# One block of attention on VectorE: the older head's output moved into the middle of a vector-matrix chunk

## The chip, the cores and the metric

The kernel runs on one core of one Trainium2 chip. The metric is the device time of one execution in microseconds, taken as the median over runs. The engines are TensorE (PE in the profile), VectorE (DVE), ScalarE (ACT), GpSimd (POOL) and the queue engine SyncE (SP); each follows its own list of instructions and waits for the others on semaphores.

## The reference, cut to what matters

Two transformer-like blocks are computed on a sequence of 512 tokens of width 1024. The change touches the attention of the first block: 16 heads of 64, causal, with a forgetting gate, and beside it a modulation vector that is a product of one vector with a large weight matrix.

```python
def forgetting_attention(q, k, v, log_f):
    ...
        logits = jnp.einsum('bqhd,bkhd->bhqk', q[:, q0:q1], k[:, :q1],
                            preferred_element_type=jnp.float32) * scale
        logits = logits + (cum[:, :, q0:q1, None] - cum[:, :, None, :q1])
        mask = jnp.arange(q0, q1)[:, None] >= jnp.arange(q1)[None, :]
        logits = jnp.where(mask, logits, -jnp.inf)
        probs = jax.nn.softmax(logits, axis=-1)
        outs.append(jnp.einsum('bhqk,bkhd->bqhd', probs.astype(v.dtype), v[:, :q1]))
    return jnp.concatenate(outs, axis=1)
...
        mod = jnp.einsum('bd,de->be', c_act, w_ada[l]) + b_ada[l]
        sh1, sc1, g1, sh2, sc2, g2 = [m[:, None, :] for m in jnp.split(mod, 6, axis=-1)]
```

## The kernel before, in words

Everything is written out by hand: each engine has its own list, and the order on it is the order of the Python code. The projections of the first block are computed with each matrix split into a high and a low part; ACT makes the high part of a weight tile (`hi`, line 745), POOL subtracts it from the raw tile to get the low part (`lo`, line 551). One weight tile is four POOL instructions of 128x512 in a row, called a burst here. TensorE then does three products per tile (lines 1705 to 1707).

The first attention is a pipeline of 18 steps, `for s in range(18)`, on every engine. In step s the heads are at different stages:

- PE first transposes the probabilities of head s-2 (`probs_t`, line 1844, ten small matmuls; before the last two it waits until the output of head s-3 has been read out of the shared bank). Then it computes a projection tile for a later pair of heads (24 matmuls, lines 1705 to 1707), then the product of probabilities and values of head s-2 (`values`, lines 1854 to 1861), then waits for the four exponentials of head s-1, sums the columns of the finished modulation chunk (`late_columns`, line 1819, in steps that follow a chunk) and computes the scores of head s (lines 2037 and 2038). Steps 14 to 17 have a part of the output projection in place of a projection tile, and it waits for the last query and key splits.
- ACT copies the transposed probabilities (line 830), computes the four exponentials of head s-1 (line 792), which need the negated row maxima from DVE, and in even steps below 14 makes the high part of the next weight tile; the POOL burst follows that. In odd steps POOL has no burst. ACT also sends the reciprocals through memory to spread them over partitions (`send_inverse`, `fetch_inverse`).
- DVE begins with the mask and the row maxima of head s-1 (lines 1460, 1177 and 1181), then the low part of a query or key tile (lines 1446 and 1449). In the steps of `LATE_STEP` it then sums a chunk of the modulation product (`weigh`, one multiply on line 1264 and seven multiply-adds on line 1270, each of 128x256 and reading two tiles of the on-chip memory, `arena` and `tmp`). In the middle of the chunk, ahead of the fourth multiply-add from the end, it takes the reciprocal of the row sums of head s-1 (`inverse`, line 1188). The last work of a step is the output of head s-2 (`output`, line 1195): two multiplies of 64x256, each reading the product from a bank and the spread reciprocals from the arena. It waits for `values` of the same step and for the reciprocals.

The steps with a chunk are 1, 2, 3, 5 to 11 and 13; steps 4, 12 and 14 on have none. Below, the middle of a chunk is the point right behind line 1188, and its second half the four multiply-adds after it.

Of the kernel before, what the change touches and what calls it, by code (L numbers as in the profile page):

```python
# [115 lines left out]
LATE_STEP = (1, 2, 3, 5, 6, 7, 8, 9, 10, 11, 13)  # L116
# [22 lines left out]
def build(nc, x, c, w_ada, b_ada, w_in, conv_w, conv_b, dt_bias, a_log, d_skip, ssm_norm_w, f_bias,  # L139
# [3 lines left out]
    with ExitStack() as ctx:  # L143
# [204 lines left out]
        def own(half):  # L348

            return slice(HD * half, HD * half + HD)  # L350
# [5 lines left out]
        def by_query(features, side):  # L356

            return features.rearrange("p (q n) -> p q n", q=TB)[:, (slice(0, 4, 3), slice(1, 3))[side]]

        def inverse_rows(h, side):  # L360

            rows_ = (inv_row if h < 16 else inv_row2)[own(h % 2)]
            return rows_.rearrange("p (n q) -> p q n", q=TB)[:, (slice(0, 4, 3), slice(1, 3))[side]]

        def value_out(side):

            return bank[3][own(side), 256:512].rearrange("p (q n) -> p q n", q=2)

        def att_pair(h):

            return att[:, h // 2] if h < 16 else att2[:, h // 2 % 2]
# [773 lines left out]
        def _(dve):  # L1145
# [37 lines left out]
            def inverse(h):  # L1183

                dve.wait_ge(p_made, 4 * h + 4)
                if h:
                    dve.wait_ge(inv_out, 16 * h)
                dve.reciprocal(rinv[:, 1], rsum[:, h % 2]).then_inc(inv_made, 1)

            def output(h):  # L1190

                dve.wait_ge(o_mm, h + 1)
                dve.wait_ge(inv_in, 16 * (h + 1))
                for side in range(2):
                    last = dve.tensor_tensor(by_query(att_pair(h)[own(h % 2)], side), value_out(side), inverse_rows(h, side), ALU.mult)
                last.then_inc(o_made, 1)

            def att_low(pair):

                dve.wait_ge(a_hi_made, T_ATT + pair + 1)  # L1200
                dve.scalar_tensor_tensor(a_lo[0][:, pair], att[:, pair], v1[:, V_ATT + pair:V_ATT + pair + 1],
                                         a_hi[0][:, pair].bitcast(F32), ALU.mult, ALU.subtract).then_inc(a_lo_made, 1)
# [57 lines left out]
            def weigh(acc, src, before, signal, middle=None, between=None):  # L1260

                for wait in before:
                    dve.wait_ge(*wait)
                link(dve.tensor_scalar(acc, src(0), cact[:, 0:1], None, ALU.mult))
                for k in range(1, KT):
                    if k == KT // 2 and middle:
                        dve.wait_ge(*middle)
                    if k == KT // 2 and between is not None:
                        inverse(between)
                    ins = dve.scalar_tensor_tensor(acc, src(k), cact[:, k:k + 1], acc, ALU.mult, ALU.add)  # L1270
                    if k < KT - 1:
                        link(ins)
                    else:
                        ins.then_inc(signal, 1)

            def late_ada(n, between=None):

                before = [(late_in[n % 2], 16 * (n // 2 + 1))] + ([(col_mm, 4 + n - 3)] if n >= 4 else [])
                weigh(late_place(n), lambda k: late_slot(n)[:, 256 * k:256 * k + 256], before, late_sum, between=between)

            def start():
                dve.wait_ge(c_made, 1)
                weigh(tmp[:, 0], lambda k: ada[:, 0, k], [(ada_half[0], 16)], ada_sum, (ada_half[1], 16))
                dve.wait_ge(vecs_t, 1)
                dve.tensor_copy(vec[:].rearrange("p a b -> p (a b)"), bank[7][:, 0:256]).then_inc(vecs_made, 1)
                dve.wait_ge(vecs_made, 1)
                for n in range(1, 4):
                    before = [(ada_in[n], 16)] + ([(col_mm, n - 1)] if n >= 2 else [])
                    weigh(tmp[:, n % 2], lambda k: ada[:, n, k], before, ada_sum)
                dve.wait_ge(col_mm, 4)  # L1290
                dve.tensor_tensor(mod[:, 0:8], bank[7][:, 256:264], v0[:, V_BADA:V_BADA + 8], ALU.add)
                dve.scalar_tensor_tensor(mod[:, 8:16], bank[7][:, 264:272], 1.0, v0[:, V_BADA + 8:V_BADA + 16], ALU.add, ALU.add).then_inc(mod_made, 1)
                dve.wait_ge(landed[U_XBC % 2], 16)
                for half in range(2):
                    cols = slice(1024 * half, 1024 * half + 1024)
                    dve.tensor_copy(w_hi[:, U_XBC % 2, cols], raw[:, U_XBC % 2, cols]).then_inc(w_hi_made, 1)
                split_affine(M_H, 0, lambda k: mod[:, 8 + k:9 + k])

            def late_mod():
                link(dve.tensor_scalar(mod[:, 16:24], mod[:, 16:24], 1.0, None, ALU.add))  # L1300
                link(dve.tensor_scalar(mod[:, 32:48], mod[:, 32:48], 1.0, None, ALU.add))

                for n, factor in ((48, mod[:, 32:40]), (64, v1[:, V_N1:V_N1 + KT])):
                    for m in range(2):
                        v = V_LN[(n - 48) // 16] + KT * m
                        link(dve.tensor_tensor(mod[:, n + KT * m:n + KT * m + KT], v1[:, v:v + KT], factor, ALU.mult))
                dve.tensor_tensor(mod[:, 56:64], mod[:, 56:64], mod[:, 24:32], ALU.add).then_inc(late_made, 1)
# [131 lines left out]
            def split_lo(n, b):  # L1439

                for half in range(2):
                    rows_ = own(half)
                    dve.wait_ge(qk_hi, 4 * n + 2 * half + 2)
                    if n % 2:
                        hc, lh = k_pair(n // 2, half)
                        dve.tensor_tensor(lh[rows_], bank[b][rows_, :], hc[rows_].bitcast(F32), ALU.subtract).then_inc(qk_lo, 1)
                    else:
                        hh, l1 = q_pair(n // 2, half)
                        dve.scalar_tensor_tensor(l1[rows_], bank[b][rows_, :], HD ** -0.5, hh[rows_].bitcast(F32),
                                                 ALU.mult, ALU.subtract).then_inc(qk_lo, 1)  # L1450

            def fox_maxima(h):

                dve.wait_ge(s_mm, h + 1)
                if h == 14:
                    dve.wait_ge(col_mm, 4 + N_LATE)
                    link(dve.tensor_tensor(mod[:, 16:48], bank[6][:, ADA_COL:ADA_COL + 32], v0[:, V_BADA + 16:V_BADA + 48], ALU.add))
                for b, o, n in ((4, 256, 2), (6, 128, 1), (5, 384, 1)):
                    diagonal = bank[b][:, o:o + n * P].rearrange("p (a k) -> p a k", a=n)
                    last = dve.tensor_tensor(diagonal, diagonal, hide.unsqueeze(1).broadcast_to([P, n, P]), ALU.add)  # L1460
                link(last)
                maxima(h, lambda q: bank[SB[q][0]][:, SB[q][1]:SB[q][1] + (q + 1) * P])
# [76 lines left out]
            for s in range(18):  # L1539
                if 1 <= s < 17:  # L1540
                    fox_maxima(s - 1)
                if 3 <= s < 15:
                    split_lo(s + 1, (s - 1) % 2)
                if s == 15:
                    for pair in range(3):
                        att_low(pair)
                elif s == 16:
                    late_mod()
                if s in LATE_STEP:
                    late_ada(LATE_FIRST + LATE_STEP.index(s), s - 1)  # L1550
                elif 1 <= s < 17:
                    inverse(s - 1)
                if s == 16:
                    att_low(3)
                    att_low(4)
                elif s == 17:
                    att_low(5)
                if s >= 2:
                    output(s - 2)
            att_low(6)  # L1560
            att_low(7)
# [700 lines left out]
```

## Time and profile before

| | |
|---|---|
| median of 3 runs | 1418.73 us (1417.94 to 1420.17) |
| the profiled execution's own time | 1418.4 us |
| its span in the trace | 1416.7 us |
| mean granted TensorE clock | 0.996 of full speed |
| PE busy | 1367.4 us, 97% of the span |
| DVE busy | 695.4 us, 49% |
| ACT busy | 547.0 us, 39% |
| POOL busy | 692.1 us, 49% |

Times are in microseconds from the start of the span. The attention of the first block lies between 257 and 430 us. The time of the execution is 1.7 us more than its span; the median of the runs is 0.3 us more than the profiled execution's time.

### The profile page before, as it was taken

What the parts mean: (1) busy time and instruction counts of PE and PEld (TensorE: products, weight loads), DVE (VectorE), ACT (ScalarE), POOL (GpSimd) and SP (SyncE); (2) the same over time, 40 slices, a digit from 0 to 9 for tenths busy, and PEclk for the clock granted to TensorE, in tenths of its full rate; (3) what the DMA queues carried; (4) which work ended last, traced back from release to release, by engine and by line L of the source; (5) the groups of instructions that cost most, each with busy time, mean ns of one, the idle gap of its engine ahead of it and who ended that gap; (6) DMA issues with size and microseconds to landing.
All of it is one profiled execution on the core that took longest, in us unless ns stands there. A gap on an engine that the chain in (4) does not pass through costs nothing.

```text
span 1416.7 us, 17285 instructions
## 1 busy us (share of the span) xinstructions
PE 1367.4 (97%) x6567; PEld 1122.0 (79%) x6567; DVE 695.4 (49%) x1005; ACT 547.0 (39%) x793; POOL 692.1 (49%) x544
## 2 busy tenths in 40 slices
PE   2999999999999999999999997999999999999999
PEld 2888778878778778888888886887788888888887
DVE  6676978689843672131324447348623213132231
ACT  0635454566663252231332316325525323142230
POOL 0453864332346664455445554753644445445442
PEclk9999999999999999999999999999999999999999
DMA  9353435745323423322232232243132322322231
GB/s 334 118 122 109 100 122 176 216 134 162 105 72 122 148 90 101 107 89 89 90 117 89 89 104 76 97 124 92 45 119 64 115 89 89 112 95 89 89 104 74
DMA packets 132248, 158.58 MB, mean 112 GB/s; under 512 B 9468, under 2 KB 93712, under 8 KB 131936
## 3 DMA queue, kind: packets, MB, share of 16 engines
q1 hardware_dynamic: 123760, 146.95, 32.9%
q10 hardware_dynamic: 6240, 5.40, 1.8%
q0 software_dynamic: 2192, 5.49, 1.2%
q8 instruction: 34, 0.56, 0.2%
q14 instruction: 22, 0.18, 0.0%
HBM read 153.47 MB, written 2.26 MB: 110 GB/s over the span
## 4 chain that ended last, share of the span: by engine, by line
PE 86%; DVE 7%; POOL 3%; issue 2%; ACT 1%; DMA 1%; SPq 0%; DVEq 0%; ACTq 0%; POOLq 0%
PE bank L1705 26%; PE bank L1707 25%; PE bank L1706 25%; POOL w_lo L551 3%; DVE tmp L1270 2%; PE bank L1844 1%; PE bank L2222 1%; DMA arena<-in_w_ada_dram 1%; PE bank L1854 1%; PE bank L1829 1%; PE bank L2037 1%; PE bank L1819 1%; PE bank L1857 1%; PE bank L2038 1%; PE bank L1981 1%
## 5 line engine op out<-in xcount | busy, mean ns | idle before, releaser
L551 POOL TENSOR_TENSOR w_lo<-raw,w_hi 128x512 fp32r<-128x512 f32 x428 | 589.9, 1410 | 593.7 <-ACT w_hi L745 592.5
L1705 PE MATMUL bank<-w_hi,a_hi 128*128 128x512 f32 x928 | 364.6, 393 | 8.5 <-DVE a_lo L1163 6.0
L1707 PE MATMUL bank<-w_hi,a_lo 128*128 128x512 f32 x928 | 361.9, 390 | 0.0
L1706 PE MATMUL bank<-w_lo,a_hi 128*128 128x512 f32 x928 | 361.9, 390 | 0.0
L745 ACT ACTIVATE w_hi<-raw 128x2048 fp32r<-128x2048 f32 x107 | 204.7, 1914 | 360.9 <-PE bank L1707 357.9
L1705 PE MATMUL bank<-a_hi,w_hi 128*128 128x512 f32 x800 | 315.6, 394 | 3.4 <-DVE a_lo L1163 2.5
L1706 PE MATMUL bank<-a_lo,w_hi 128*128 128x512 f32 x800 | 312.1, 390 | 0.0
L1707 PE MATMUL bank<-a_hi,w_lo 128*128 128x512 f32 x800 | 312.0, 390 | 0.0
L1705 PEld LDWEIGHTS bank<-w_hi,a_hi 128*128 128x128 f32 x928 | 174.7, 188 | 46.4 <-DVE a_lo L1163 6.2
L1707 PEld LDWEIGHTS bank<-w_hi,a_lo 128*128 128x128 f32 x928 | 174.6, 188 | 36.8
L1706 PEld LDWEIGHTS bank<-w_lo,a_hi 128*128 128x128 f32 x928 | 174.7, 188 | 35.5
L1705 PEld LDWEIGHTS bank<-a_hi,w_hi 128*128 128x128 f32 x800 | 150.6, 188 | 35.5 <-issue 2.7
L1707 PEld LDWEIGHTS bank<-a_hi,w_lo 128*128 128x128 f32 x800 | 150.6, 188 | 32.0
L1706 PEld LDWEIGHTS bank<-a_lo,w_hi 128*128 128x128 f32 x800 | 150.7, 188 | 30.5 <-issue 0.2
L1251 DVE TENSOR_TENSOR tmp<-arena 128x512 f32<-128x512 f32 x64 | 64.3, 1005 | 190.1 <-ACT arena L843 190.0
L843 ACT ACTIVATE arena<-bank 128x512 f32<-128x512 f32 x64 | 38.4, 599 | 211.1 <-PE bank L1707 204.7
L1694 DVE SCALAR_TENSOR_TENSOR arena<-bank,st,arena 128x512 f32<-128x512 f32 x32 | 24.0, 751 | 144.6 <-PE bank L1707 144.6
L1270 DVE SCALAR_TENSOR_TENSOR tmp<-arena,cact,tmp 128x256 f32<-128x256 f32 (+1 forms) x140 | 88.0, 629 | 4.7
L1151 DVE TENSOR_TENSOR a_lo<-tmp,a_hi 128x512 fp32r<-128x512 f32 x64 | 67.6, 1057 | 7.2
L1593 DVE TENSOR_TENSOR arena<-bank,arena 128x512 f32<-128x512 f32 x24 | 16.6, 692 | 109.6 <-PE bank L1707 109.6
L792 ACT ACTIVATE arena<-bank,mxs 128x128 f32<-128x128 f32 (+1 forms) x96 | 49.5, 534 | 35.0 <-DVE mxs L1181 35.0
L845 ACT ACTIVATE a_hi<-arena 128x512 fp32r<-128x512 f32 x64 | 40.5, 633 | 2.0
(248 smaller groups left out, 1246.7 us busy)
## 6 DMA issues: line engine op xcount, KB each, us to landing
raw<-in_w_mlp_dram SPq DMA_DIRECT2D x32, 1024.0 KB, 5.2
raw<-in_w_in_dram SPq DMA_DIRECT2D x24, 1024.0 KB, 5.2
arena<-in_w_ada_dram SPq DMA_DIRECT2D x18, 1024.0 KB, 6.5
raw<-in_w_ff_in_dram SPq DMA_DIRECT2D x16, 1024.0 KB, 5.4
raw<-in_w_ff_out_dram SPq DMA_DIRECT2D x16, 1024.0 KB, 5.0
raw<-in_w_out_dram SPq DMA_DIRECT2D x12, 1024.0 KB, 5.5
raw<-in_w_in_dram SPq DMA_DIRECT2D x16, 512.0 KB, 6.0
arena<-in_w_ada_dram SPq DMA_DIRECT2D x3, 2048.0 KB, 18.0
```

Of the source, the lines that this page charges most:

```text
L551: last = pool.tensor_tensor(w_lo[:, u0 % 2, cols], raw[:, u0 % 2, cols], w_hi[:, u0 % 2, cols].bitcast(F32), ALU.subtract)
L745: act.activation(w_hi[:, u0 % 2], raw[:, u0 % 2], ACT.Copy).then_inc(w_hi_made, 1)
L792: act.activation(dst[:, QO[q]:QO[q] + n], src(q), ACT.Exp, bias=mxs[:, h % 2, q:q + 1], accum_out=rsum[:, h % 2, q:q + 1]).then_inc(p_made, 1)
L843: act.activation(rl[:, k % 2], bank[4 * b + j][:], ACT.Relu).then_inc(evac[b], 1)
L845: act.activation(a_hi[1][:, k], rl[:, k % 2], ACT.Square).then_inc(a_hi_made, 1)
L1151: dve.tensor_tensor(a_lo[buf][:, k], tmp[:, m0 % 2], a_hi[buf][:, k].bitcast(F32), ALU.subtract)\
L1251: dve.tensor_tensor(tmp[:, k % 2], rl[:, k % 2], rl[:, k % 2], ALU.mult).then_inc(tile_made, 1)
L1270: ins = dve.scalar_tensor_tensor(acc, src(k), cact[:, k:k + 1], acc, ALU.mult, ALU.add)
L1694: dve.scalar_tensor_tensor(x1[:, t, part], bank[4 * b + t][:], st[:, 12 + t:13 + t], x1[:, t, part], ALU.mult, ALU.add).then_inc(evac[b], 1)
L1705: pe.matmul(out_, hi_a, hi_b, start=start, stop=False)
L1706: pe.matmul(out_, hi_a, lo_b, start=False, stop=False)
L1707: return pe.matmul(out_, lo_a, hi_b, start=False, stop=stop)
```

## The change

The output of head s-2 moves within step s on DVE: in a step with a chunk it now stands in the middle of the chunk, behind the reciprocals of head s-1, and no longer behind the chunk. In steps without a chunk it stays where it was. `inverse(between)` is called with `between` = s-1, so `output(between - 1)` is `output(s - 2)`; in step 1 there is nothing to put out. No instruction is added or removed, no other engine's list changes, and no tile changes its place.

```diff
@@ -1267,6 +1267,8 @@
                         dve.wait_ge(*middle)
                     if k == KT // 2 and between is not None:
                         inverse(between)
+                        if between:
+                            output(between - 1)
                     ins = dve.scalar_tensor_tensor(acc, src(k), cact[:, k:k + 1], acc, ALU.mult, ALU.add)
                     if k < KT - 1:
                         link(ins)
@@ -1555,7 +1557,7 @@
                     att_low(4)
                 elif s == 17:
                     att_low(5)
-                if s >= 2:
+                if s >= 2 and s not in LATE_STEP:
                     output(s - 2)
             att_low(6)
             att_low(7)
```

Below is DVE's order from the middle of the chunk in step 2 to the row maxima that open step 3, before the change (line 1270 is the multiply-add, 1195 the output, 1460 the mask of step 3).

```order
L1188 RECIPROCAL rinv<-rsum 128x4
L1270 SCALAR_TENSOR_TENSOR tmp<-arena,cact,tmp 128x256 x4
L1195 TENSOR_TENSOR arena<-bank,arena 64x2x128
L1195 TENSOR_TENSOR arena<-bank,arena 64x256
L1460 TENSOR_TENSOR bank<-bank,masks 128x256
```

The same stretch of DVE after the change, where the lines behind the edit carry numbers that are two higher.

```order
L1188 RECIPROCAL rinv<-rsum 128x4
L1195 TENSOR_TENSOR arena<-bank,arena 64x2x128
L1195 TENSOR_TENSOR arena<-bank,arena 64x256
L1272 SCALAR_TENSOR_TENSOR tmp<-arena,cact,tmp 128x256 x4
L1462 TENSOR_TENSOR bank<-bank,masks 128x256
```

The two output multiplies went ahead of the second half of the chunk; steps 3, 5 to 11 and 13 read the same way.

The second place is DVE after the change from the reciprocal of step 12, which has no chunk, to the maxima that open step 14 (line 1451 and 1448 are the query and key splits).

```order
L1188 RECIPROCAL rinv<-rsum 128x4
L1195 TENSOR_TENSOR arena<-bank,arena 64x2x128
L1195 TENSOR_TENSOR arena<-bank,arena 64x256
L1462 TENSOR_TENSOR bank<-bank,masks 128x256
L1462 TENSOR_TENSOR bank<-bank,masks 128x128 x2
L1177 TENSOR_REDUCE rinv<-bank 128x1 x4
L1181 TENSOR_SCALAR mxs<-rinv 128x4
L1451 SCALAR_TENSOR_TENSOR q_split<-bank,q_split 64x512 x2
L1264 TENSOR_SCALAR tmp<-arena,cact 128x256
L1272 SCALAR_TENSOR_TENSOR tmp<-arena,cact,tmp 128x256 x3
L1188 RECIPROCAL rinv<-rsum 128x4
L1195 TENSOR_TENSOR arena<-bank,arena 64x2x128
```

In step 12 nothing moved; in step 13 the output stands in the chunk again, ahead of the maxima of step 14 and the key split on which PE's step 14 waits.

## Rows read from the trace of the kernel before

**Rows 1.** The first line of the page: busy time of each engine.

```profile
PE 1367.4 (97%) x6567; PEld 1122.0 (79%) x6567; DVE 695.4 (49%) x1005; ACT 547.0 (39%) x793; POOL 692.1 (49%) x544
```

**Rows 2.** By stretch: length, busy PE, PEld, DVE, ACT, POOL, granted clock, DMA share, GB/s.

```profile
257.00:304.00 47.00, 47.00 (x282) 38.93 (x283) 37.35 (x91) 30.01 (x72) 14.91 (x17) 1.00 0.59 159
304.00:365.00 61.00, 58.97 (x363) 48.07 (x362) 58.22 (x128) 40.23 (x94) 18.93 (x19) 1.00 0.56 169
```

**Rows 3.** Waits of PE between 257 and 430 us: total, times, longest.

```profile
PE bank L1844 <- DVE arena L1195: 1.9, 2, 1.5
PE bank L1705 <- DVE k_split L1446: 0.8, 1, 0.8
PE bank L1844 <- ACT arena L830: 0.5, 2, 0.3
```

**Rows 4.** DVE's timeline, steps 6 to 10: start, duration, instruction.

```profile
310.52 3.99 DVE L1270 SCALAR_TENSOR_TENSOR tmp<-arena,cact,tmp 128x256 f32<-128x256 f32 x4
...
315.80 0.83 DVE L1460 TENSOR_TENSOR bank<-bank,masks 128x256 f32<-128x256 f32 x3
...
321.93 2.02 DVE L1270 SCALAR_TENSOR_TENSOR tmp<-arena,cact,tmp 128x256 f32<-128x256 f32 x4
...
325.25 0.83 DVE L1460 TENSOR_TENSOR bank<-bank,masks 128x256 f32<-128x256 f32 x3
...
331.29 0.18 DVE L1188 RECIPROCAL rinv<-rsum 128x4 f32<-128x4 f32 x1
331.38 2.96 DVE L1270 SCALAR_TENSOR_TENSOR tmp<-arena,cact,tmp 128x256 f32<-128x256 f32 x4
...
345.13 0.83 DVE L1460 TENSOR_TENSOR bank<-bank,masks 128x256 f32<-128x256 f32 x3
```

**Rows 5.** POOL's timeline: bursts of steps 2 and 8.

```profile
272.41 5.19 POOL L551 TENSOR_TENSOR w_lo<-raw,w_hi 128x512 fp32r<-128x512 f32 x4 [14.18 <-ACT w_hi L745]
...
332.79 5.20 POOL L551 TENSOR_TENSOR w_lo<-raw,w_hi 128x512 fp32r<-128x512 f32 x4 [6.50 <-ACT w_hi L745]
```

**Rows 6.** DVE's timeline ahead of the attention: whole chunks of seven.

```profile
219.89 7.28 DVE L1270 SCALAR_TENSOR_TENSOR tmp<-arena,cact,tmp 128x256 f32<-128x256 f32 x7
...
235.89 3.61 DVE L1270 SCALAR_TENSOR_TENSOR tmp<-arena,cact,tmp 128x256 f32<-128x256 f32 x7
```

**Rows 7.** POOL's timeline in the same stretch.

```profile
220.63 5.74 POOL L551 TENSOR_TENSOR w_lo<-raw,w_hi 128x512 fp32r<-128x512 f32 x4 [7.91 <-ACT w_hi L745]
```

**Rows 8.** DVE's timeline, step 2 and the opening of step 3.

```profile
270.62 0.18 DVE L1188 RECIPROCAL rinv<-rsum 128x4 f32<-128x4 f32 x1 [0.45 <-ACT arena L792]
...
273.20 1.22 DVE L1195 TENSOR_TENSOR arena<-bank,arena 64x256 f32<-64x256 f32 x2 [0.47 <-PE bank L1857]
275.10 0.83 DVE L1460 TENSOR_TENSOR bank<-bank,masks 128x256 f32<-128x256 f32 x3 [0.68 <-PE bank L2038]
```

**Rows 9.** PE's timeline, steps 2, 3, 7 and 13, single instructions.

```profile
271.85 0.43 PE L1854 MATMUL bank<-arena 128*64 128x256 f32 x1
...
281.54 0.43 PE L1854 MATMUL bank<-arena 128*64 128x256 f32 x1
...
282.77 0.27 PE L1819 MATMUL bank<-ones,tmp 128*128 128x1 f32 x1
...
322.96 0.38 PE L1819 MATMUL bank<-ones,tmp 128*128 128x1 f32 x2
...
380.86 0.43 PE L1854 MATMUL bank<-arena 128*64 128x256 f32 x1
```

**Rows 10.** ACT's timeline: exponentials of step 7, weight tile of step 8.

```profile
318.58 0.37 ACT L792 ACTIVATE arena<-bank,mxs 128x128 f32<-128x128 f32 x1 [1.84 <-DVE mxs L1181]
...
320.51 0.21 ACT L792 ACTIVATION_READ_ACCUMULATOR arena<-bank,mxs 128x1 f32 x1
...
330.76 1.95 ACT L745 ACTIVATE w_hi<-raw 128x2048 fp32r<-128x2048 f32 x1
```

**Rows 11.** DVE's timeline, step 13.

```profile
380.90 0.18 DVE L1188 RECIPROCAL rinv<-rsum 128x4 f32<-128x4 f32 x1
```

## The prediction

> **What bounds the kernel now.** I read the page first, for the balance of the engines: PE is busy for 97% of the span [rows 1], so a change matters by what it adds to or takes from PE's waits. The change stands in the first attention alone, so next came the busy time by stretch. From 304 to 365 us, the steps 6 to 11, PE is busy 58.97 of 61 us and DVE 58.22 [rows 2]. The reader is to see that DVE is as full there as PE: the two bound this stretch together. From 257 to 304 us PE has no gap at all. Then came PE's waits from 257 to 430 us [rows 3]. They are 3.2 us in all: 1.9 for an output of DVE (line 1195), 0.8 for a key split of DVE, 0.5 for a copy by ACT. That is the most that any better order on DVE can give back here.
>
> Then I read DVE's timeline. A step begins with the row maxima: at 315.80 in step 7, 325.25 in step 8 and 345.13 us in step 10 [rows 4]. So the odd step 7 takes 9.45 us, and the two steps 8 and 9 take 19.88, the even one of them 10.43 if step 9 is like step 7. PE's own step is 9.69 us (values of step 2 at 271.85, of step 3 at 281.54) [rows 9]. Two steps of DVE, 19.88 us, are longer than two of PE, 19.38. The even steps are longer because their second half of a chunk takes 2.96 us (step 8) or 3.99 (step 6) where the odd step 7 needs 2.02 [rows 4]. What stands beside it is POOL: in step 8 its burst starts at 332.79 [rows 5], inside the second half that runs from 331.38 to 334.34.
>
> **The price of a burst to a chunk.** Ahead of the attention there are whole chunks with and without a burst. Seven multiply-adds take 3.61 us alone and 7.28 with a burst of four across them [rows 6, 7]. So a held multiply-add costs (7.28 - 3.61) / 4 = 0.92 more, 1.44 in place of 0.52. The output is not held: it took 1.22 us at 273.20, in the midst of the burst of 272.41 to 277.60 [rows 5, 8].
>
> The Trainium skill has a rule that speaks against this change ("SBUF — State Buffer", section on the two separate sides): DVE and GpSimd share a pair of ports as a lock and not as bandwidth, and a DVE instruction with two inputs in that memory waits out a running GpSimd instruction. The trace agrees, 1.44 us in place of 0.52, also in that the output, with one input in a bank, is free. By the rule alone each held multiply-add would wait for what is left of one POOL instruction, about the same sum.
>
> **The change part by part.** It adds and removes nothing. It moves ten outputs of 1.22 us (1.26 with the gap) ahead of four multiply-adds. That does two things: the output now waits in the chunk where PE's product isn't there yet, and the second half starts 1.26 us later or more, which in the even steps is into POOL's burst.
>
> Where the burst lies, relative to the maxima of an even step: the exponentials start 2.78 behind the maxima (315.80 to 318.58), the weight tile on ACT 2.0 behind that, the burst 2.03 after it (330.76 to 332.79) [rows 4, 5, 10], so 6.8 us in all when ACT waits for nothing else. The middle of the chunk is 6.22 behind the maxima (331.29 + 0.18 - 325.25) [rows 4], the second half now 7.5. So the burst starts 0.7 us ahead of the second half, and all four multiply-adds are held: the first for the rest of a quarter of a burst, about 0.9, three at 1.44, in all 5.2 us.
>
> Step 2. The middle is reached at 270.80, but PE only begins the values at 271.85 and the output can start 1.35 later, at 273.20, as now [rows 8, 9]. It ends at 274.42, and the second half starts in a burst that ends near 277.9: one at 0.9, two at 1.44, one free, 4.3 us. The maxima of step 3 start at 278.8 and not at 275.10 [rows 8]. The exponentials end 4.9 behind the maxima (315.80 to 320.72) [rows 4, 10], at 283.7. PE wants them at 282.77 [rows 9]: a new wait, **+0.9 us**. Queued behind it are the scores of head 3, and DVE's next maxima wait for these. Step 4 has no chunk, so DVE catches up, but PE's 0.9 stays.
>
> Step 5, like step 13: in step 13 the middle is reached at 381.08, PE begins the values at 380.86 and the output can start at 382.2 [rows 9, 11]. DVE stands for 1.1 us. It enters step 6 later by 0.9 + 1.1 = 2.0.
>
> Step 6: the second half takes 5.2 in place of 3.99, so the maxima of step 7 come 3.2 to 3.3 later, at 319.1, and the exponentials end at 324.0. PE would be there at 322.96, less the 1.5 us that it now waits for the output in this step [rows 3], which is gone since the output comes early, plus 0.9: at 322.4. It waits until 324.0, so it stands **+1.1 us** behind today. The gain that the move can have is in this term, and the maxima eat it.
>
> Steps 8 and 10: from here PE follows DVE, since scores need exponentials and these the maxima. Two steps of DVE take 19.88 - 2.96 + 5.2 = 22.1 us. That is 2.2 more than now, twice: **+4.4 us**. In both, PE's wait moves from the output (even steps) to the exponentials (line 792, odd steps).
>
> Steps 12 to 14: step 12 has no chunk and DVE catches up with PE again. In step 13 it stands 1.1 us for the values, so the key split in step 14 comes 1.1 later, and PE waits for that split already (0.8 us, [rows 3]). **+1.0 us**, a tenth less for a short wait at the opening of step 14 that this covers.
>
> Sum: 1.1 (which holds the 0.9 of step 3) + 4.4 + 1.0 = 6.5 us. Behind step 14 PE is the bound again and waits for little, so nothing gives the loss back. Against the profiled execution's 1418.4 us this is 1424.9; the median of the runs shown is 0.3 above that execution, so I say **1425.2 us**.
>
> Bounds of the one unknown, the second half under a burst (the trace has none of four held in an even step). From below: no more than it costs now, 3.99 and 2.96. Then DVE's two steps stay at 19.88 and only the 1.1 waits count: PE is about 1.0 ahead at step 7 (1.5 gained, 0.5 waited) and loses 1.0 in step 14, so 0.0 to +0.5. From above: four whole quarters, 4 x 1.44 = 5.8. Then each even step has 0.6 more, step 2 too, some 2 us in all: +8.5. I take 5.2, as the chunk of [rows 6] is the same instruction under the same burst.
>
> **The rivals.**
> - *No difference.* The second half in a burst costs no more than now, since POOL starts later or in other gaps. Against it: all four fall behind the start of the burst by rows. Time 1418.7 to 1419.2. Chance 0.10.
> - *Faster.* PE's waits for the output (1.9), the split (0.8) and ACT's copy (0.5) all vanish: 1415.5 us. It is one mechanism: the early output frees the shared bank before PE wants it, while DVE's later maxima stay within the slack of the exponentials. That slack is 322.96 - 320.72 = 2.2 us in step 7, less the 1.5 that PE gains [rows 9, 10]; so the maxima may be 0.7 late at most, and that is where it decides. By my sum they are 3.3 late. Chance 0.03.
> - *Slower, but half.* Only two of four are held in steps 6 to 10 (3.9 us): two steps of DVE take 20.8, PE loses 0.9 twice, and little in step 7, so some +2.5, 1421.2. What would speak for it is that POOL starts later than by rows. Chance 0.12.
> - *Slower, all four at full price*, 1427.2 us. Chance 0.10.
> - *The forecast*, 1423 to 1426.5 by itself. Chance 0.65.
>
> **How the numbers follow.** The predicted time is the forecast's. The range takes in the half case's upper side and the full price, 1421.3 to 1427.5, and leaves out some 0.18. About 0.2% (2.8 us) is what a measurement of this kernel can tell from no change: so slower by more than that holds the forecast, the full price and half of the half case, 0.82; within it 0.15; faster 0.03.
>
> **What the changed profile would show.** From 304 us on, DVE's second halves in steps 6, 8 and 10 at 5.2 us or near it, and in step 2 at 4.3 (now 2.02). Maxima of odd steps 3 us and more behind today's, with 22 us from step 7 to step 9. PE's waits for line 1195 gone, and in their place waits of 1.5 to 3 us ahead of lines 1819 and 2037 for ACT's line 792 in steps 7, 9 and 11, 0.9 in step 3. A wait of near 2 us for the key split in step 14. DVE idle for 1.1 us ahead of line 1195 in steps 5 and 13 and 2.4 in step 2. Behind 400 us, all shifted by one amount. The prediction is wrong if the second halves stay under 4 us, or if PE's waits for the exponentials stay under 1 us.

## The result and the profile after

The change makes the kernel slower by 0.8%: 1430.01 us (1428.53 to 1431.11, 4 runs) against 1418.40 us (1417.94 to 1420.17), ratio 1.0079 [1.0068, 1.0091]. The profiled execution took 1428.53 us. The same kernel timed again beside the one before gave 1428.24 us against 1418.47, ratio 1.0067 [1.0053, 1.0081] (e12_after_again below). So the loss is 9.8 to 11.6 us where 6.8 was forecast, and both medians lie above the range.

The first lines of the page, for [rows 1]:

```profile
span 1426.8 us, 17285 instructions
PE 1370.0 (96%) x6567; PEld 1125.4 (79%) x6567; DVE 706.5 (50%) x1005; ACT 547.9 (38%) x793; POOL 694.5 (49%) x544
```

The same instructions on every engine, 10.1 us more span, and 11.1 us more busy time on DVE though no work was added to it. Grouped by line, DVE's instructions between 257 and 440 us, first before and then after the change (line, engine, operation, shapes, count | busy us, mean ns | idle before):

```profile
L1270 DVE SCALAR_TENSOR_TENSOR tmp<-arena,cact,tmp 128x256 f32<-128x256 f32 x77 | 40.9, 531 | 2.4
L1195 DVE TENSOR_TENSOR arena<-bank,arena 64x256 f32<-64x256 f32 x32 | 19.6, 611 | 15.4 <-PE bank L1857 14.9
```

```profile
L1272 DVE SCALAR_TENSOR_TENSOR tmp<-arena,cact,tmp 128x256 f32<-128x256 f32 x77 | 48.6, 632 | 2.5
L1195 DVE TENSOR_TENSOR arena<-bank,arena 64x256 f32<-64x256 f32 x32 | 19.5, 610 | 21.8 <-PE bank L1859 21.4
```

The multiply-adds of the chunks alone cost 7.7 us more; DVE stands 21.8 us ahead of the output, where it stood 15.4. PE's waits in the same stretch, for [rows 3]:

```profile
PE bank L1821 <- ACT arena L792: 7.0, 4, 2.8
PE bank L1707 <- DVE k_split L1448: 3.3, 1, 3.3
PE bank L1846 <- DVE arena L1195: 0.4, 1, 0.4
```

The wait for the output has gone from 1.9 to 0.4 us, and 7.0 us of waits for the exponentials have come. DVE's timeline of steps 2 and 6 to 10 after the change, for [rows 4, 8]:

```profile
273.18 1.22 DVE L1195 TENSOR_TENSOR arena<-bank,arena 64x256 f32<-64x256 f32 x2 [2.40 <-PE bank L1859]
274.33 4.25 DVE L1272 SCALAR_TENSOR_TENSOR tmp<-arena,cact,tmp 128x256 f32<-128x256 f32 x4
...
313.84 5.27 DVE L1272 SCALAR_TENSOR_TENSOR tmp<-arena,cact,tmp 128x256 f32<-128x256 f32 x4
319.14 0.83 DVE L1462 TENSOR_TENSOR bank<-bank,masks 128x256 f32<-128x256 f32 x3
...
326.66 2.05 DVE L1272 SCALAR_TENSOR_TENSOR tmp<-arena,cact,tmp 128x256 f32<-128x256 f32 x4
328.74 0.83 DVE L1462 TENSOR_TENSOR bank<-bank,masks 128x256 f32<-128x256 f32 x3
...
336.18 5.22 DVE L1272 SCALAR_TENSOR_TENSOR tmp<-arena,cact,tmp 128x256 f32<-128x256 f32 x4
341.44 0.83 DVE L1462 TENSOR_TENSOR bank<-bank,masks 128x256 f32<-128x256 f32 x3
```

POOL's bursts beside the two held halves, for [rows 5]:

```profile
313.25 5.58 POOL L551 TENSOR_TENSOR w_lo<-raw,w_hi 128x512 fp32r<-128x512 f32 x4 [7.38 <-ACT w_hi L745]
...
335.56 5.57 POOL L551 TENSOR_TENSOR w_lo<-raw,w_hi 128x512 fp32r<-128x512 f32 x4 [8.08 <-ACT w_hi L745]
```

The burst starts 0.6 us ahead of the second half in steps 6 and 8, and all four multiply-adds of it are held: 5.27 and 5.22 us. The odd step 7 has none beside it, 2.05. The maxima of step 7 start at 319.14, 3.34 us behind [rows 4], and those of step 9 come 22.30 us after them. PE's row at the end of step 7's wait, for [rows 9]:

```profile
324.13 0.61 PE L1821 MATMUL bank<-ones,tmp 128*128 128x1 f32 x4 [2.14 <-ACT arena L792]
```

That is 1.17 us behind the 322.96 of before. Up to here the prediction holds to 0.2 us. What it didn't have begins with the granted clock. By stretch, for [rows 2] (us, busy PE, PEld, DVE, ACT, POOL, granted clock, DMA share, GB/s), first before and then after:

```profile
343.00:352.00 9.00, 9.00 (x53) 7.49 (x55) 8.58 (x21) 6.98 (x16) 1.06 (x2) 1.00 0.43 133
367.00:376.00 9.00, 9.00 (x58) 7.46 (x57) 4.92 (x13) 8.75 (x20) 3.47 (x3) 1.00 0.09 19
394.00:402.00 8.00, 8.00 (x48) 6.50 (x47) 5.03 (x13) 5.11 (x15) 0.00 (x0) 1.00 0.53 151
```

```profile
343.00:352.00 9.00, 6.19 (x37) 5.48 (x34) 8.51 (x20) 4.25 (x12) 1.06 (x2) 0.81 0.69 237
367.00:376.00 9.00, 7.70 (x43) 6.72 (x40) 8.51 (x21) 5.45 (x14) 1.05 (x2) 0.81 0.50 178
394.00:402.00 8.00, 4.75 (x16) 3.49 (x15) 4.44 (x9) 7.13 (x15) 4.96 (x4) 0.79 0.05 5
```

0.81 over 9 us, and 0.79 over 8, are 3.4 us at TensorE's lower level, 1.2 GHz, and the rest at 2.4. They begin at 346.8, 370.6 and 398.0 us: the first two 0.3 and 1.9 us behind the end of PE's waits in steps 9 and 11, the third 0.5 us ahead of the end of its wait in step 14. Before the change there is none in the attention. The second thing stands at the opening of step 14, on DVE and on POOL:

```profile
393.25 0.83 DVE L1462 TENSOR_TENSOR bank<-bank,masks 128x256 f32<-128x256 f32 x3
...
395.84 1.21 DVE L1181 TENSOR_SCALAR mxs<-rinv 128x4 f32<-128x4 f32 x1
396.96 1.40 DVE L1448 TENSOR_TENSOR k_split<-bank,k_split 64x512 fp32r<-64x512 f32 x2
```

```profile
395.76 4.96 POOL L551 TENSOR_TENSOR w_lo<-raw,w_hi 128x512 fp32r<-128x512 f32 x4 [3.07 <-ACT w_hi L745]
```

```profile
398.41 0.79 PE L1707 MATMUL bank<-w_hi,a_hi 128*128 128x512 f32 x1 [3.25 <-DVE k_split L1448]
```

The negation of the maxima, four elements a row, takes 1.21 us. The burst began 0.08 us ahead of it and holds it, and the key split, for which PE waits, is queued behind. Before the change the negation was over before the burst came:

```profile
386.90 0.17 DVE L1181 TENSOR_SCALAR mxs<-rinv 128x4 f32<-128x4 f32 x1
```

```profile
388.06 5.01 POOL L551 TENSOR_TENSOR w_lo<-raw,w_hi 128x512 fp32r<-128x512 f32 x4 [3.08 <-ACT w_hi L745]
```

But the trace of before has the same hold at another place, where it could have been read ahead of the change. Step 4 has no chunk, and the negation that opens step 5 comes so early that it runs into the last quarter of step 4's burst: it takes 0.60 us and ends with that quarter, near 297.65. The one that opens step 13, behind step 12 without a chunk, takes 0.60 us too.

```profile
297.07 0.60 DVE L1181 TENSOR_SCALAR mxs<-rinv 128x4 f32<-128x4 f32 x1
```

```profile
292.61 5.04 POOL L551 TENSOR_TENSOR w_lo<-raw,w_hi 128x512 fp32r<-128x512 f32 x4 [6.52 <-ACT w_hi L745]
```

The table is PE's lateness against the kernel before, in us, and the experiments are read by it. It is the start of PE's first score matmul of steps 7, 11 and 13 (line 2039 after the change), and of its first value matmul of step 14, less the same start in the trace of before; each trace is shifted so that the values of step 2 fall together. The stretches at 1.2 GHz are those in the attention, each 3.4 us long. In e4_clean_after the value matmul of step 14 falls into the stretch; once that is over, PE is 2.5 us late.

| kernel | step 7 | 11 | 13 | 14 | at 1.2 GHz, near | median less its before |
|---|---|---|---|---|---|---|
| after | 1.19 | 6.09 | 7.73 | 11.37 | 347, 371, 398 | +11.6 |
| after, again (e12) | 1.14 | 6.01 | 7.65 | 11.27 | 346, 370, 398 | +9.8 |
| e3_fill | 1.17 | 6.02 | 6.02 | 9.88 | 397 | +9.0 |
| e8_fill_all | 1.15 | 5.99 | 5.99 | 8.29 | none | +9.0 |
| e6_s14 | 1.20 | 6.16 | 7.81 | 10.62 | 326, 370, 397 | +9.7 |
| e13_fill_s14 | 1.13 | 5.97 | 5.97 | 7.23 | none | +8.1 |
| e10_only13 | 0 | 0 | 0 | 3.60 | 389 | +2.9 |
| e1_even | 2.24 | 7.91 | 9.84 | 9.37 | 329 | +9.6 |
| e2_odd | 2.43 | 9.53 | 9.53 | 11.80 | 317, 341, 365 | +12.2 |
| e4_clean_after | -1.88 | -1.90 | -1.36 | 2.15 | 390 | +1.9 |
| e5_clean_before | -1.88 | -2.85 | -2.85 | -3.31 | none | -3.0 |
| e9_clean_after_s14 | -1.35 | -0.99 | -0.35 | 0.89 | none | +0.6 |
| e11_wait | 2.30 | 8.19 | 8.19 | 8.21 | 326, 350 | +8.3 |

### The profile page after: what moved, and what is told of

It reads as the page before. It is cut to its first block, busy times and chain, and to the rows that moved or that the text cites. A ratio compares the mean times of both kernels' runs of the same rounds, so it can differ in the third digit from the quotient of the medians.

```text
span 1426.8 us, 17285 instructions
## 1 busy us (share of the span) xinstructions
PE 1370.0 (96%) x6567; PEld 1125.4 (79%) x6567; DVE 706.5 (50%) x1005; ACT 547.9 (38%) x793; POOL 694.5 (49%) x544
## 4 chain that ended last, share of the span: by engine, by line
PE 84%; DVE 9%; POOL 3%; issue 2%; ACT 2%; DMA 1%; SPq 0%; DVEq 0%; POOLq 0%; ACTq 0%
PE bank L1707 25%; PE bank L1709 25%; PE bank L1708 25%; DVE tmp L1272 3%; POOL w_lo L551 3%; PE bank L1846 1%; DMA arena<-in_w_ada_dram 1%; PE bank L2224 1%; PE bank L1831 1%; DVE rinv L1177 1%; PE bank L1856 1%; DVE arena L1195 1%; PE bank L1859 1%; PE bank L1821 1%; PE bank L1983 1%
## 5 line engine op out<-in xcount | busy, mean ns | idle before, releaser
L1272 DVE SCALAR_TENSOR_TENSOR tmp<-arena,cact,tmp 128x256 f32<-128x256 f32 (+1 forms) x140 | 95.8, 684 | 4.8
L1195 DVE TENSOR_TENSOR arena<-bank,arena 64x256 f32<-64x256 f32 x48 | 29.3, 610 | 28.1 <-PE bank L1859 27.5
```

## The experiments

Line numbers shift by up to twelve with the edits; the words of a row tell the instruction.

**e1_even and e2_odd: half of the change each.** One table picks the steps in which the output stands in the chunk; e1_even has the steps 2, 6, 8 and 10, e2_odd has 3, 5, 7, 9, 11 and 13.

```diff
+MOVED = (2, 6, 8, 10)
...
-                        if between:
+                        if between and between + 1 in MOVED:
                             output(between - 1)
...
-                if s >= 2 and s not in LATE_STEP:
+                if s >= 2 and s not in MOVED:
                     output(s - 2)
```

> The output stands in the middle of the chunk in the even steps 2, 6, 8 and 10 alone; in the odd ones it stays behind the chunk. Burst theory (multiply-adds held by POOL's bursts are the cost, and bursts come in even steps alone): the second halves of steps 6, 8 and 10 take 5.2 us as in the changed kernel, and an odd step is no shorter than now, so the loss is all there: 1427 to 1431 us. Rival (the cost is DVE standing in the chunk for PE's product, in steps 3, 5 and 13 as much as in step 2): only step 2 still waits, so most of the loss goes, 1420 to 1422 us.

Measured: 1428.14 us (1427.78 to 1430.01), ratio 1.0068 [1.0054, 1.0082]. PE's waits between 257 and 440 us:

```profile
PE bank L1847 <- DVE arena L1196: 5.9, 5, 1.7
PE bank L1822 <- ACT arena L793: 4.6, 4, 1.3
```

The even half has the held second halves (4.76 us in steps 6 and 8), and in odd steps the output stays last and is now late by them, so PE waits for it, 5.9 us. Both kinds of wait stand side by side, and it loses 1.8 us more up to step 11 than the whole change.

> The output stands in the middle of the chunk in the odd steps 3, 5, 7, 9, 11 and 13 alone, where POOL has no burst. Burst theory in its plain form: no multiply-add is newly held, so only the 1.1 us waits of steps 5 and 13 count: 1419 to 1421 us. A less plain form: DVE comes later into each even step by that wait, its second half meets more of the burst (3 held in place of 1 or 2) and PE waits both for the output in even steps and for the exponentials in odd ones: up to 1425 us. Rival (standing for PE's product is the cost): six of the ten moves are here, so more than half of the 11 us stays.

Measured: 1430.81 us (1429.27 to 1431.88), ratio 1.0087 [1.0073, 1.0101]. PE's waits, and then rows of DVE's timeline:

```profile
PE bank L1847 <- DVE arena L1196: 7.6, 4, 2.7
PE bank L1708 <- DVE k_split L1449: 3.3, 1, 3.3
```

```profile
312.02 3.81 DVE L1273 SCALAR_TENSOR_TENSOR tmp<-arena,cact,tmp 128x256 f32<-128x256 f32 x4
315.85 1.21 DVE L1196 TENSOR_TENSOR arena<-bank,arena 64x256 f32<-64x256 f32 x2
...
325.78 1.23 DVE L1196 TENSOR_TENSOR arena<-bank,arena 64x256 f32<-64x256 f32 x2 [2.47 <-PE bank L1860]
```

I had thought this half nearly free, as no burst lies in odd steps, and had allowed 1425 us at most. It is as slow as the whole change, and that theory falls; what holds for this half is the rival, that DVE stands for PE's product. PE opens the odd step with a wait for the output that DVE still puts last in the even step; its values are late by it; DVE, which now wants these values in the middle of the odd chunk, stands 2.47 us, the rest of its chunk and the next even step come later by it, and so does the output for which PE waits next. The two engines wait for each other in turn. And the burst still reaches two multiply-adds of the even chunk, 3.81 us in steps 6, 8 and 10 (3.99, 2.96 and 2.96 before). All multiply-adds together take only 1.7 us more than before, so in this half it is the stands, with the stretches at 1.2 GHz beside them, and not the held instructions that make PE 9.5 us late at step 11:

```profile
L1273 DVE SCALAR_TENSOR_TENSOR tmp<-arena,cact,tmp 128x256 f32<-128x256 f32 x77 | 42.6, 553 | 2.6
```

So the odd and the even half of the move aren't two parts of a sum: each is dearer alone, and the whole change is cheaper than either up to step 11.

> The output in the middle in odd steps once more, one look for the place of its half-clock stretches: as in its first run if the stretches are tied to PE's waits.

The kernel that ran under this label is that of e2_odd, line for line, so it is a second execution of it, 1433.62 us: 9.47 us late at step 11, 13.00 at step 14, with a fourth stretch at 1.2 GHz near 403 us. It tells nothing else.

**e3_fill and e8_fill_all: the clock apart from the waits.** PE gets matmuls that nobody reads, into a bank that is free, just ahead of its waits, so that it is busy there and still can't go on earlier. e3_fill has them in steps 3, 7, 9 and 11, e8_fill_all also at the opening of step 14 (the loop over 11, which e3_fill hasn't). They add work that the reference doesn't have.

```diff
+FILL = {3: 3, 7: 8, 9: 11, 11: 11}
...
+                for m in range(11 if s == 14 else 0):
+                    pe.matmul(bank[7][:], w_hi[:, 1, 0:P], a_hi[0][:, m % KT], start=True, stop=True)
                 if s >= 2:
                     probs_t(s - 2, prob)
...
+                for m in range(FILL.get(s, 0)):
+                    pe.matmul(bank[7][:], w_hi[:, 0, 0:P], a_hi[0][:, m % KT], start=True, stop=True)
                 if 1 <= s < 16:
                     pe.wait_ge(p_made, 4 * s)
```

> The changed kernel, with 3, 8, 11 and 11 extra matmuls of 128x512 (0.23 us each, into a bank that is free there) on PE ahead of its wait for the exponentials in steps 3, 7, 9 and 11, where PE stands for 0.8 to 2.8 us; what they compute is overwritten. Clock theory (the half-clock stretches at 347, 371 and 398 us follow PE's idle time and carry some 4 us of the loss): with PE kept busy the first two go away and the time falls by 2.5 to 3 us, to about 1427, although PE does more. Rival (the clock is no part of it, the waits alone are the loss): no gain, 1430 or up to 1 us more where a filler outlasts a wait.

> The changed kernel with extra matmuls ahead of PE's waits in steps 3, 7, 9 and 11 as before, and 11 more at the opening of step 14, where PE later stands 3.3 us for the key split; what they compute is overwritten. Clock theory: no half-clock stretch is left in the attention, and the time is that of the waits alone: the 6.5 us of the forecast plus 1.0 for the held negation in step 14, 1425 to 1426.5. Rival (filling one place only moves the stretch elsewhere, or PE is late by the fillers): 1427.5 as with four places, or above.

Measured: e3_fill 1427.51 us (1425.52 to 1430.00), ratio 1.0065 [1.0052, 1.0079]; e8_fill_all 1427.87 us (1426.10 to 1430.21), 1.0064 [1.0050, 1.0078]. By stretch, e3_fill:

```profile
367.00:376.00 9.00, 8.89 (x49) 7.38 (x48) 8.54 (x21) 5.29 (x14) 1.05 (x2) 1.00 0.46 153
394.00:402.00 8.00, 5.78 (x27) 4.24 (x27) 2.31 (x4) 4.96 (x14) 4.53 (x4) 0.79 0.27 56
```

and e8_fill_all:

```profile
394.00:402.00 8.00, 7.26 (x44) 5.56 (x44) 3.39 (x6) 4.80 (x13) 4.43 (x4) 1.00 0.28 58
```

With the filler the clock stays at 1.00 behind the waits, and PE's lateness at step 11 is what it was (6.02 and 5.99, 6.09 without). But from step 11 to 13 nothing is lost any more, where the change lost 1.64 us, and step 14 loses 2.30 us in e8_fill_all where e3_fill loses 3.86. So the stretch near 371 us costs 1.6 us and the one near 398 costs 1.6; the one near 347 costs 0.1 at most, because DVE is the bound there and PE would have waited anyway. The medians don't show all of it: e8_fill_all's whole kernel is no faster than e3_fill's, and slower than the 1425 to 1426.5 us expected. In its profiled execution the 1.2 GHz stretch behind the next layer norm, near 506 us, is 6.8 us long and not 3.4, and the end is 0.9 us later than the lateness at step 14 and the earlier start of its trace (0.65 us) account for.

**e6_s14 and e13_fill_s14: the held negation.** POOL's burst at the opening of step 14 waits until DVE has the negation of that step; e13_fill_s14 has this and all the filler.

```diff
+                if u == U_WO1 + 1:
+                    pool.wait_ge(mx_made, 14)
                 lo(u)
```

> The changed kernel, with POOL's burst of step 14 alone held back until the maxima of head 13 are negated. In the changed kernel that burst starts 0.08 us ahead of the negation (line 1181), which then takes 1.21 us and not 0.17, and PE waits for the key split behind it. If that hold is a term of the loss, the time falls by 1.0 us, or by 2 to 2.5 if the shorter wait of PE also saves the half-clock stretch at 398 us. If the key split is late for DVE's chunk alone: no change beyond 0.3 us.

> The changed kernel with all extra matmuls (steps 3, 7, 9, 11 and 14) and POOL's burst of step 14 behind the negation. If the loss in the attention is the sum of held multiply-adds and DVE's wait in step 13 (8.3 us by the version with fillers alone, less 1.0 for the held negation) and the rest is clock, PE is 7.2 to 7.5 us behind the kernel before at the end of the attention, with no half-clock stretch between 260 and 430 us; 1425 to 1427 us, the later stretches as they fall. If the two terms aren't apart (the negation's hold hides under something else), 8.3 us.

Measured: e6_s14 1427.74 us (1426.01 to 1428.26), ratio 1.0064 [1.0050, 1.0078]; e13_fill_s14 1426.53 us (1424.02 to 1427.05), 1.0051 [1.0037, 1.0065], beside 1428.24 for the change. DVE and POOL in e6_s14:

```profile
395.50 0.17 DVE L1183 TENSOR_SCALAR mxs<-rinv 128x4 f32<-128x4 f32 x1
```

```profile
395.75 4.98 POOL L551 TENSOR_TENSOR w_lo<-raw,w_hi 128x512 fp32r<-128x512 f32 x4 [3.40 <-DVE mxs L1183]
```

The negation is back at 0.17 us, the wait for the key split goes from 3.3 to 2.2 us, and between e8_fill_all and e13_fill_s14, which differ in this alone, PE's lateness falls by 1.06 us. What is left, 7.23, is 5.97 up to step 11 and 1.26 in step 14. DVE's stand in step 13 is 0.80 us of these 1.26; most of the rest is the negation that opens step 13, 0.94 us under the end of a burst where it took 0.60 before.

**e10_only13: the move in one step.** `MOVED = (13,)`.

> The output in the middle of the chunk in step 13 alone. The forecast's term for it: DVE stands 1.1 us for PE's product and the key split of step 14 comes that much later, +1.0 us. With the held negation of step 14, as in the changed kernel, +2.0, and with a half-clock stretch behind PE's longer wait up to +3.5: 1420.5 to 1422. Without either: 1419.5.

Measured: 1421.74 us (1419.89 to 1422.91), ratio 1.0021 [1.0012, 1.0030]. PE's wait and the clock, 384 to 393 us:

```profile
PE bank L1708 <- DVE k_split L1449: 3.3, 1, 3.3
```

```profile
384.00:393.00 9.00, 5.75 (x20) 4.34 (x19) 5.74 (x13) 8.25 (x18) 5.01 (x5) 0.81 0.06 16
```

Ten outputs moved cost 11.4 us by the end of the attention, and one of them alone costs 3.6: the same wait of 3.3 us, the negation again at 1.21 us, the same stretch at 1.2 GHz, which begins 0.5 us ahead of the wait's end. No second half is held longer here. It is the term of step 13 with both of its unforeseen followers, in a kernel that is otherwise on time.

**e4_clean_after, e5_clean_before and e9_clean_after_s14: bursts out of DVE's way.** POOL's bursts of steps 2 to 12 wait for the end of DVE's chunk where the step has one, and the last quarter of each for the negated maxima; e4_clean_after is the changed kernel with this, e5_clean_before the kernel before with it, e9_clean_after_s14 adds the condition of e6_s14.

```diff
...
+                if chunk is not None:
+                    pool.wait_ge(late_sum, chunk + 1)
                 for part in range(4):
+                    if part == 3 and head is not None:
+                        pool.wait_ge(mx_made, head + 1)
...
+                s = 2 * (u - U_QK1)
+                if 2 <= s < 14:
+                    lo(u, chunk=LATE_FIRST + LATE_STEP.index(s) if s in LATE_STEP else None, head=s)
```

> The changed kernel, with POOL's bursts of the attention moved in time: in an even step with a chunk the burst waits until the chunk is summed, and its last quarter until the next maxima are negated, so that it lies beside DVE's bank-reading work. Burst theory: the second halves go back to 2.05 us, DVE's two steps to 19 us, the new waits for the exponentials and with them the half-clock stretches go, and what is left is the 1.1 us wait of step 13: 1417.5 to 1420 us. Rival (early output and DVE's wait for PE are the cost by themselves): the loss stays over 5 us, above 1424.

> The kernel before (output behind the chunk in every step), with POOL's bursts moved in time as in the clean version of the changed kernel. Burst theory: no multiply-add is held, DVE's two steps (19 us) are shorter than PE's (19.4), PE's waits for the output in the opening of steps 7, 9 and 11 go: 1415 to 1417 us, and it is faster than its counterpart with the moved output by the 1 us that DVE stands for PE's product in step 13. Rival (PE's waits in the kernel before come from elsewhere): 1418 to 1419.

> The changed kernel with POOL's bursts moved in time and the burst of step 14 held back behind the negation as well. Burst theory: what was left of the loss with clean bursts (2 us) was this hold and the half-clock stretch at 390 us that followed the 3.2 us wait for the key split: 1417.3 to 1418.8. Rival (that rest is DVE standing for PE's product in step 13): no gain over 1420.5.

Measured: e4_clean_after 1420.46 us (1418.88 to 1423.65), ratio 1.0020 [1.0009, 1.0030]; e5_clean_before 1415.09 us (1413.77 to 1416.78), 0.9978 [0.9969, 0.9988]; e9_clean_after_s14 1419.46 us (1417.97 to 1423.27), 1.0008 [0.9999, 1.0017]. The two changed kernels are slower than expected by 0.5 and 0.7 us, and the executions of e4_clean_after fall into two groups (1418.9 to 1420.5 us and, four of nine, 1423.1 to 1423.7), so its median says less than its trace. PE's waits in e4_clean_after:

```profile
PE bank L1715 <- DVE k_split L1456: 3.2, 1, 3.2
PE bank L1854 <- DVE arena L1203: 1.2, 3, 0.4
```

With the burst behind the chunk the 7.0 us of waits for the exponentials are gone, and of the 11.4 us of lateness at step 14 2.15 are left (2.5 behind the stretch): the term of step 14 with its negation (1.21 us again) and its clock. So the overlap of second half and burst makes most of what the change loses in steps 2 to 12: PE is 7.73 us late at step 13 with it and 1.36 early without. The place of the output has a price too, since the same bursts help the kernel before more, 2.85 early at step 13. Its DVE and POOL rows:

```profile
321.51 2.02 DVE L1278 SCALAR_TENSOR_TENSOR tmp<-arena,cact,tmp 128x256 f32<-128x256 f32 x4
...
331.20 2.02 DVE L1278 SCALAR_TENSOR_TENSOR tmp<-arena,cact,tmp 128x256 f32<-128x256 f32 x4
```

```profile
333.36 3.79 POOL L555 TENSOR_TENSOR w_lo<-raw,w_hi 128x512 fp32r<-128x512 f32 x3 [6.99 <-DVE tmp L1278]
337.58 1.28 POOL L555 TENSOR_TENSOR w_lo<-raw,w_hi 128x512 fp32r<-128x512 f32 x1 [0.43 <-DVE mxs L1189]
```

A step of DVE is 9.69 us now in even and odd steps alike (321.51 to 331.20), which is PE's own; PE's waits for the output fall from 1.9 to 0.5 us, and the kernel is faster than both. With clean bursts the moved output still costs 5.4 us (1420.46 less 1415.09, two chips). In PE's lateness at step 14 it is 5.46 (2.15 and -3.31). Up to step 13 it is 1.49 of that, and step 14 adds 3.97: e4_clean_after loses 3.51 there, e5_clean_before gains 0.46. In e9_clean_after_s14, where the negation of step 14 isn't held and no stretch at 1.2 GHz follows, step 14 adds 1.70, and the steps up to 13 are 2.50. Nor are the moved bursts out of DVE's way in all places. Where the output no longer stands between the chunk and the maxima, the negation is over before the third quarter of the burst is, and the last quarter follows at once. It holds the multiply that opens the chunk in steps 3, 7, 9 and 11, 1.20 to 1.23 us each for 0.35 in e5_clean_before. Step 7 of e4_clean_after:

```profile
318.49 1.22 DVE L1272 TENSOR_SCALAR tmp<-arena,cact 128x256 f32<-128x256 f32 x1
```

DVE also waits there for the reciprocals that ACT sends through memory, 2.2 us in all in e4_clean_after and 3.3 in e9_clean_after_s14, a wait that neither e5_clean_before nor the change with its old bursts has.

**e11_wait: waits without the change.** The kernel before, in which PE waits in steps 7, 9 and 11 until DVE has put out the older head, which nothing needs there.

```diff
+                if s in (7, 9, 11):
+                    pe.wait_ge(o_made, s - 1)
```

> The kernel before, in which PE stands in steps 7, 9 and 11 ahead of the scores until DVE has put out the older head of the same step (a wait of some 1.8 us each that nothing needs). DVE's order is untouched. If PE's waits bring half-clock stretches, the trace has some between 325 and 375 us that the kernel before has not. The time then is the waits (DVE is the bound in these steps, so part of them hides: +2 to +6 us) and the stretches on top. Rival (stretches come by place, not by waits): none in the attention.

Measured: 1427.17 us (1426.01 to 1427.36), ratio 1.0054 [1.0040, 1.0068]. PE's waits, and the stretches behind two of them:

```profile
PE bank L1819 <- issue: 5.8, 3, 2.2
```

```profile
322.00:331.00 9.00, 6.75 (x41) 5.97 (x36) 5.91 (x15) 3.16 (x6) 1.06 (x2) 0.81 0.46 136
346.00:355.00 9.00, 7.29 (x35) 6.47 (x36) 6.65 (x16) 5.13 (x14) 1.05 (x2) 0.81 0.47 132
```

Three waits of 1.8 to 2.2 us bring two stretches at 1.2 GHz into a kernel that had none there, and PE is 8.2 us late at the end of 5.8 us of waits. So waits bring the lower clock, whatever causes them; it isn't something of the changed order. Which wait does it is not shown. In the changed kernel the wait of 2.14 us in step 7 has no stretch behind it, and in e6_s14 the same wait has one. e1_even has six waits of 1.3 to 1.7 us and one stretch, e9_clean_after_s14 a wait of 2.2 us and none. The wait of 3.25 us for the key split has a stretch behind it in e7_s3only and none in e2_odd, one kernel executed twice.

**e12_after_again: the change beside e13_fill_s14.**

> The changed kernel once more, beside the next one. Clock theory: half-clock stretches near 325 or 347, 371 and 398 us as in its first run, and PE 11 us behind the kernel before at the end of the attention; 1428.5 to 1431 us.

Measured: 1428.24 us (1426.01 to 1430.49). The lateness repeats that of the first profile to 0.1 us in every step, and so do the places of the three stretches. The medians of the same kernel are 1.8 us apart. Executions of one kernel differ in the number of stretches at 1.2 GHz: the two profiled ones of e2_odd's kernel have a mean granted clock of 0.993 and 0.989 and took 1429.27 and 1433.62 us. So terms of 1 us are read here from the lateness inside the traces and not from the medians.

## Why the prediction was right up to step 11 and too low behind it

- **The held second half: right.** 4.25 us in step 2 (forecast 4.3), 5.27 and 5.22 in steps 6 and 8 (forecast 5.2), by the price of the chunk of [rows 6]. Step 10 has 4.76, since DVE stood 0.59 us for the output first and the burst was further on.
- **Step 3: right**, +0.84 for 0.9. **Step 7: right**, maxima at 319.14 for 319.1, PE at 324.13 for 324.0, +1.19 for 1.1.
- **Steps 7 to 9 and 9 to 11: right, a little small.** 2.4 us each without the clock's share (e13_fill_s14: 1.13, 3.54, 5.97) for 2.2. The odd step of DVE became 9.60 us (319.14 to 328.74) for 9.45. In all 6.0 us up to step 11 for 5.5.
- **Where the waits went: right.** From the output to the exponentials (7.0 us, 4 times) and to the key split, where it is 3.3 us for a forecast of near 2; DVE stands 2.40 us for PE's product in step 2 (forecast 2.4), 0.80 in step 5 and 1.20 in step 13 (1.1 each).
- **"Step 12 has no chunk and DVE catches up with PE again": wrong by what it leaves out.** DVE does catch up, but PE runs 3.4 us at 1.2 GHz in that step, +1.6 us, which is gone with filler ahead of the wait of step 11 (e3_fill).
- **Step 14, "+1.0 us": the step that failed most.** It is 3.64 us. With neither the lower clock nor the held negation it is 1.26 (e13_fill_s14), most of it the stand of DVE in step 13 that the term meant (0.80 us there, 1.20 in the changed kernel). Two things that it left out come on top: the negation held by the burst, 1.06 (e8_fill_all against e13_fill_s14), and the stretch near 398 us, what is left of the 3.64, 1.3 (1.6 by e3_fill against e8_fill_all). I had looked only at multiply-adds as what a burst can hold, and had not asked what else on DVE would meet a burst once DVE was 9 us later and POOL only 7.7; the trace of before shows the held negation twice, at 0.60 us.
- **The sum.** Forecast 1.1 + 4.4 + 1.0 = 6.5. Found 6.1 + 1.6 + 3.6 = 11.4 us of lateness at step 14, of which the lower clock is 3 and the negation 1. "Behind step 14 nothing gives the loss back" holds up to 500 us, where PE is still 11.36 late. There both kernels have a stretch at 1.2 GHz at the wait after the layer norm. Before the change it begins 1.2 us behind the wait and falls on work alone; after the change it begins 0.3 us ahead of the wait's end, so less work is slowed (lateness 11.36 at its start, 10.70 behind it). The end of the span is 10.1 late. How many such stretches an execution has differs from run to run, and the medians of 9.8 and 11.6 us lie around that.
- **The rivals.** "No difference", "faster" and "half" fall with the rows of DVE. "All four at full price" has the time nearest to the result, 1427.2, but not its reason: its 5.8 us a half didn't come. The range was too narrow because it was built from the price of a held half alone, and no bound stood for what a new wait does to PE besides lasting.

The Trainium skill's rule on the shared ports ("SBUF — State Buffer", the section on the two separate sides) was cited in the prediction for instructions with two inputs. The same sentence of it names DVE instructions in a two-port mode as well. The trace fits that wider reading, though it doesn't show in which mode an instruction ran: the negation, one input and four elements a row, took 1.21 us in place of 0.17 under the burst, and a multiply of one input of 128x256 took 1.20 to 1.23 in place of 0.35 in e4_clean_after.

What stays open: what decides which wait is followed by a stretch at 1.2 GHz, and how the difference between moved and unmoved output under the moved bursts (e9_clean_after_s14 is 4.4 us behind e5_clean_before, measured on another chip) divides between the waits for PE's product, the held multiplies and DVE's waits for the reciprocals. No run here takes these three apart.

## What to carry to other kernels

Moving a result earlier on one engine moves whatever stood there later; before pricing the gain, lay the later part beside the other engine's bursts, and that includes the four-element instructions ahead of the split that TensorE waits for. An output that is moved ahead of its own product makes a stand in the middle of a chunk, and if the next wait of the other engine hangs on that chunk the two wait in turn, as in e2_odd. Here the burst, not the output, was what could move for free: POOL's low parts held back to the end of the chunk gave 0.2% (e5_clean_before).

## What the runs showed of the hardware that was not expected

- Single waits of PE of 1.3 to 3.3 us in a stage that is otherwise full can bring 3.4 us at 1.2 GHz: in e11_wait at two of three waits of 1.8 to 2.2 us, after the change at three of the five of 0.8 to 3.3 us, in e1_even at one of six. Such a stretch costs 1.6 us where PE is the bound and 0.1 where DVE is.
- Filler on PE ahead of the wait, 11 matmuls, kept the clock at 1.00 in steps 9, 11 and 14 and cost no lateness (6.02 us at step 11 against 6.09).
- A DVE instruction of 128x4 ends with the burst's quarter that it meets: 1.21 us for 0.17 where the quarter began 0.08 us ahead of it, 0.60 where it met the end of one.
- POOL pays less than DVE for the same overlap: a burst of four is 5.57 us with four multiply-adds held by it and 5.01 where it holds none (388.06 us before the change), 0.14 us an instruction, while a held multiply-add pays 0.8 ((5.27 - 2.05) / 4).
